# Latent and stick-breaking attention of a four-layer model reordered into one loop of heads, and the layer norms' scale and bias moved from POOL to ACT

## The reference, cut to what matters

```python
# first_block: layer 0 gated delta net + conv FFN, layer 1 short convolution + conv FFN
h = layer_norm(ALPHA * h + mix, ln_mix_g[i], ln_mix_b[i])
h = layer_norm(ALPHA * h + conv_ffn(h, ...), ln_ffn_g[i], ln_ffn_b[i])
# second_block, layer 0: mixer_mla_sb; layer 1: mixer_fox
h = x @ w_in                                   # c_q 256, c_kv 256, k_rope 32, sb_qkv 3*8*64
q  = rms_norm(c_q, q_norm_g) @ w_uq            # 8 heads of 64 + 32 (rope)
kv = rms_norm(c_kv, kv_norm_g) @ w_ukv         # 8 heads of 64 (k) + 64 (v)
o_a = softmax(q k^T * 96**-0.5, block mask) @ v        # latent attention (MLA), 8 heads
# stick-breaking (SB), 8 heads: z = q k^T / 8, past = s < t
log_rem = where(past, log_sigmoid(-z), 0); between = reverse_cumsum(log_rem) - log_rem
o_b = where(past, exp(log_sigmoid(z) + between), 0) @ v
mix = concatenate([o_a, o_b]) @ w_out
x = layer_norm(DEEPNORM_ALPHA * x + mix, ...); x = layer_norm(DEEPNORM_ALPHA * x + swiglu(x), ...)
x = x + sigmoid(x @ ple_w_gate + ple_b_gate) * (p @ ple_w_proj)
```

## Time and profile before

| | |
|---|---|
| median of 3 runs | 1532.27 us (1530.16 to 1534.51) |
| profiled execution, its own time | 1531.54 us |
| its span, first to last instruction | 1529.7 us |
| mean granted TensorE clock | 0.973 of full speed |
| busy: PE, DVE, ACT, POOL | 1428.1, 1062.2, 917.5, 416.3 us |
| attention stage, 777.6 to 910.9 us | 133.3 us |
| one weight unit from issue to landing | 3.7 us (median of 419) |

### The profile page before, as it was taken

The page is one execution under the profiler, slowest core; times in us unless marked ns, Lnnn a source line. Parts: engine busy times, 40 slices in busy tenths (PEclk is TensorE's granted clock), DMA queues, the critical chain, the costliest instruction groups (busy, mean ns, idle before and its releaser), DMA issues.

```text
span 1529.7 us, 30955 instructions
## 1 busy us (share of the span) xinstructions
PE 1428.1 (93%) x11068; PEld 1370.9 (90%) x11068; DVE 1062.2 (69%) x1682; ACT 917.5 (60%) x1535; POOL 416.3 (27%) x427
## 2 busy tenths in 40 slices
PE   6989988999999999999988789999998989999997
PEld 6889978999999999998977669999998968999997
DVE  7776645888748978886487627765567755866557
ACT  5622345555685475557756657556865876655864
POOL 4122000632205306322062004512037020722005
PEclk9989998999999999999999899999999999999999
DMA  5422214455564564555635105655645532555562
GB/s 202 148 73 87 66 52 128 129 176 179 158 203 136 175 196 145 171 180 176 199 120 163 58 14 163 197 178 179 200 144 152 168 108 84 179 178 192 181 191 83
DMA packets 62725, 226.00 MB, mean 148 GB/s; under 512 B 6960, under 2 KB 8240, under 8 KB 62640
## 3 DMA queue, kind: packets, MB, share of 16 engines
q1 hardware_dynamic: 61776, 221.87, 46.9%
q10 hardware_dynamic: 864, 3.01, 0.6%
HBM read 223.80 MB, written 1.05 MB: 147 GB/s over the span
## 4 chain that ended last, share of the span: by engine, by line
PE 61%; DVE 22%; issue 6%; ACT 6%; POOL 3%; DMA 1%; DVEq 1%; SPq 0%; ACTq 0%
PE bank L393 16%; PE bank L394 16%; PE bank L395 16%; DVE w_lo L1536 8%; DVE cv L1894 2%; POOL h L2164 2%; DVE x_lo L1572 1%; ACT w_hi L1034 1%; DVE r L1631 1%; POOL h L2162 1%; ACT unused L1021 1%; DVE tu L1596 1%; DVE tg L1596 1%; DVE r L1576 1%; PE bank L903 1%
## 5 line engine op out<-in xcount | busy, mean ns | idle before, releaser
L393 PE MATMUL bank<-x_hi,w_hi 128*128 128x258 f32 (+5 forms) x2144 | 621.1, 290 | 31.0 <-DVE w_lo L1536 15.7
L395 PE MATMUL bank<-x_hi,w_lo 128*128 128x258 f32 (+5 forms) x2144 | 611.1, 285 | 0.0
L394 PE MATMUL bank<-x_lo,w_hi 128*128 128x258 f32 (+5 forms) x2144 | 611.1, 285 | 0.0
L393 PEld LDWEIGHTS bank<-x_hi,w_hi 128*128 128x128 f32 x2144 | 409.1, 191 | 40.3 <-issue 20.6
L1536 DVE TENSOR_TENSOR w_lo<-raw,w_hi 128x1024 fp32r<-128x1024 f32 x299 | 392.1, 1325 | 49.1 <-ACT w_hi L1034 34.6
L394 PEld LDWEIGHTS bank<-x_lo,w_hi 128*128 128x128 f32 x2144 | 409.8, 191 | 0.5
L395 PEld LDWEIGHTS bank<-x_hi,w_lo 128*128 128x128 f32 x2144 | 409.2, 191 | 0.0
L1034 ACT ACTIVATE w_hi<-raw 128x1024 fp32r<-128x1024 f32 x299 | 313.4, 1053 | 120.0 <-PE bank L395 100.9
L1534 DVE SCALAR_TENSOR_TENSOR w_lo<-raw,negmean,w_hi 128x1024 fp32r<-128x1024 f32 x120 | 155.5, 1299 | 151.8 <-ACT w_hi L1032 150.6
L393 PE MATMUL bank<-a_hi,w_hi 128*128 (+2 forms) x704 | 199.1, 283 | 6.2 <-DVE w_lo L1534 6.1
L395 PE MATMUL bank<-a_hi,w_lo 128*128 (+2 forms) x704 | 198.8, 282 | 0.0
(11 more groups left out here) (410 smaller groups left out, 2169.7 us busy)
## 6 DMA issues: line engine op xcount, KB each, us to landing
raw<-w SPq DMA_DIRECT2D x419, 512.0 KB, 3.7
h<-h SPq DMA_DIRECT2D x2, 544.0 KB, 6.6
out<-h SPq DMA_DIRECT2D x8, 128.0 KB, 1.9
T<-cs ACTq DMA_DIRECT2D x1, 960.0 KB, 5.1
con_b<-cb ACTq DMA_DIRECT2D x1, 712.0 KB, 4.1
smx<-pin ACTq DMA_DIRECT2D x1, 512.0 KB, 5.0
con_g<-ca ACTq DMA_DIRECT2D x1, 421.5 KB, 8.0
prm<-par ACTq DMA_DIRECT2D x1, 202.0 KB, 4.6
```

Source lines behind the costliest of these rows:

```text
L393: pe.matmul(o, wh, xh, start=first, stop=False)
L394: pe.matmul(o, wh, xl, start=False, stop=False)
L395: return pe.matmul(o, wl, xh, start=False, stop=last)
```

## The change

It has two parts.

**The attention stage.** The kv latent comes before the q latent in `m_in` and in the norms, and `m_ukn` before `m_uq` (host-side order of the weights). x3 is written to buffers of its own, `y3_hi` and `y3_lo`; POOL scales its tiles 4 to 7 (`ln_times`) and DVE 0 to 3, in the order `X3_ORDER`. The split of p (`p_hi`, `p_lo`) moves from before the stage to the start of norm 1. The rope of k comes after the low halves, its copy to eight heads goes from DVE to POOL; the latents' deviations, reciprocals and splits move between the q and k units. `m_sbv` is accumulated in `misc[0..1]`, so v is copied from there; `m_ukn` and `m_uq` go into half banks, k is copied by DVE in four operations, q by ACT in four, and q's rope is three DVE operations for four heads (`q_ropes`). The two attentions become one loop: round i has the scores of MLA head i+1, the sums of SB head i+1, z of SB head i+2, the value product of SB head i, the transpose of MLA head i and the value product of MLA head i-1. SB uses `misc[0..1]` and `acc[0..1]`, MLA `misc[2]` (scores), `misc[3]` (transpose) and `acc[2..3]`. The first units of `m_out` are averaged and split within the loop, and `row_stage(4)` takes the tiles in the order `M_ORDER`, in which they are finished. One activation table serves both attentions and is loaded in the q and k units.

**The layer norms.** `keep` on POOL makes only `r * rstd`. Scale and bias are an ACT activation, `gain_and_bias`, at fixed places: two in each of the first four pairs of an up phase, two in each of the first four tiles of the short convolution, one in each gate unit. In `pair` on ACT the row mean moves behind the first tap.

The diff, cut to its core:

```diff
 (PE)
-            first_pair(U["m_sbqk"], SEQ, "x3", list(range(KT)), U["m_sbqk"] - 3)
...
-            panels(U["m_sbqk"] + 2, 6, SEQ)
+            first_pair(U["m_sbqk"], SEQ, "x3", X3_ORDER, U["m_sbqk"] - 3, y3)
+            c_sums(0)
+            panels(U["m_sbqk"] + 2, 2, SEQ, None, y3)
+            c_sums(1)
+            panels(U["m_sbqk"] + 4, 4, SEQ, None, y3)
             mean_of_h(4, SEQ)
+            pe.wait_ge(S("c_std"), 2)
+            tokens(U["m_sbv"], KT, y3_hi, y3_lo, misc)
+            four(U["m_ukn"], c_hi[:, 0:2, :], c_lo[:, 0:2, :], halves_of(misc[2:4]))
...
+            four(U["m_uq"], c_hi[:, 2:4, :], c_lo[:, 2:4, :], halves_of(acc[0:2]))
+            four(U["m_uq"] + 1, c_hi[:, 2:4, :], c_lo[:, 2:4, :], halves_of(acc[2:4]))
+            sb_z(0)
+            pe.wait_ge(S("k_copied"), 1)
+            tokens(U["m_ukv"], 2, c_hi[:, 0:2, :], c_lo[:, 0:2, :], misc[2:4])
+            sb_z(1)
+            sb_sums(0)
+            pe.wait_ge(S("k_rope"), 1)
+            mla_scores(0)
+            for i in range(9):
+                if i + 1 < 8:
+                    mla_scores(i + 1)
+                    sb_sums(i + 1)
+                if i + 2 < 8:
+                    sb_z(i + 2)
+                if i < 8:
+                    sb_times_v(i)
+                    mla_turn(i)
+                if i:
+                    mla_times_v(i - 1)
+            row_stage(4, SEQ, mixed)
 (ACT)
+            def gain_and_bias(n, k, N):
+                scaled_n[0] += 1
+                act.wait_ge(S("ln_h1"), scaled_n[0])
+                A(h[:, k, 0:N], h[:, k, 0:N], ACT.Identity, bias=par_col(f"ln_b{n}", k), scale=par_col(f"ln_g{n}", k)).then_inc(S("ln_h"), 1)
...
                 def pair(u, s, j):
                     act.wait_ge(S("unit_done"), u + 1)
-                    ahead(u, s)
+                    split(u + RING, s + RING)
                     act.wait_ge(S("ffn_tu"), jb + 1)
...
                         A(cv[:, par, 0:M], tu[:, par, 0:M], ACT.Copy, scale=par_col(conv, j * 3)).then_inc(S("ffn_tap0"), 1)
+                        row_mean(u + (RING + 1), s + RING + 1)
                         act.wait_ge(S("ffn_taps"), j + (cbase + 1))
...
                     ahead(u + 1, s + 1)
+                    if isinstance(j, int) and j < KT // 2:
+                        gain_and_bias(2 * ups[0], 2 * j, N)
+                        gain_and_bias(2 * ups[0], 2 * j + 1, N)
...
+            for i in range(9):
+                if i + 1 < 8:
+                    sb_soft(i + 1)
+                if i < 8:
+                    mla_exp(i)
+                    sb_att(i)
+                if 1 <= i < 4:
+                    row_mean(U["m_out"] + i, U["m_out"] + i)
+                    split(U["m_out"] + i, U["m_out"] + i)
+                if i == 4:
+                    row_mean(U["m_out"] + 4, U["m_out"] + 4)
+                if i:
+                    mla_copy(i - 1)
+                if i >= 2 and i % 2 == 0:
+                    sb_high(i // 2 - 1)
+                if i >= 3 and i % 2:
+                    mla_high(i // 2 - 1)
...
                     if i == 0 and m >= 2:
                         y_copy(m - 2)
+                    gain_and_bias(n, m, SEQ)
                     act.wait_ge(S("gate_t"), KT * i + m + 1)
 (DVE)
+            def q_ropes(j):
+                q, t = q_m[:, 4 * j:4 * j + 4, :], q_t[:, 4 * j:4 * j + 4, :]
...
+                dve.wait_ge(S("q_copied"), j + 1)
+                link(V.tensor_tensor(t[rope_rows], q[swap_rows], turn(swap_rows), ALU.mult))
+                link(V.tensor_tensor(q[rope_rows], q[rope_rows], turn(rope_rows), ALU.mult))
+                V.tensor_tensor(q[rope_rows], q[rope_rows], t[rope_rows], ALU.add).then_inc(S("q_rope"), 1)
...
+            q_ropes(0)
+            sb_remains(0)
+            mla_max(0)
+            for i in range(9):
+                if i + 1 < 8:
+                    sb_remains(i + 1)
+                if i < 8:
+                    mla_norm(i)
+                if i == 0:
+                    q_ropes(1)
+                if 1 <= i < 4:
+                    ahead(U["m_ukn"] + i, U["m_ukn"] + i)
+                if i + 1 < 8:
+                    mla_max(i + 1)
+                if i >= 2 and i % 2 == 0:
+                    mixed_low(4 + i // 2 - 1, acc[(i // 2 - 1) % 2])
+                if i >= 3 and i % 2:
+                    mixed_low(i // 2 - 1, acc[2 + (i // 2 - 1) % 2])
 (POOL)
             def keep(n, k, N):
                 G.tensor_tensor(h[:, k, 0:N], r[:, k, 0:N], rstd[:, 0:N], ALU.mult).then_inc(S("ln_h1"), 1)
-                pool.wait_ge(S("ln_h1"), KT * kept[0] + k + 1)
-                G.tensor_scalar(h[:, k, 0:N], h[:, k, 0:N], par_col(f"ln_g{n}", k), par_col(f"ln_b{n}", k), ALU.mult, ALU.add).then_inc(S("ln_h"), 1)
...
+            for k in range(4, KT):
+                G.tensor_tensor(r[:, k, 0:SEQ], r[:, k, 0:SEQ], rstd[:, 0:SEQ], ALU.mult).then_inc(S("ln_times"), 1)
+            for k in range(4, KT):
+                pool.wait_ge(S("ln_times"), k - 3)
+                G.tensor_scalar(h[:, k, 0:SEQ], r[:, k, 0:SEQ], par_col("ln_g3", k), par_col("ln_b3", k), ALU.mult, ALU.add).then_inc(S("ln_h"), 1)
...
+            G.tensor_copy(k_m[64:96, :, :], rope_t[64:96, 0, :].unsqueeze(1).to_broadcast([32, 8, SEQ])).then_inc(S("k_rope"), 1)
```

More of the change, by code:

```diff
@@ L300, in v_banks, with halves_of @@
             return [acc[first % RING], acc[(first + 1) % RING]]
+        def halves_of(pair):
+            return [pair[m // 2][:, (m % 2) * SEQ:(m % 2) * SEQ + SEQ] for m in range(4)]
         def blocks(t, lv, side):
@@ L1259, in up_phase @@
                 act.preload_act_table_set("silu_and_others")
-                with act.Fori(0, 6) as i:
+                for j in range(KT // 2):
+                    pair(u0 + 2 * j, u0 + 2 * j, j)
+                with act.Fori(0, 4) as i:
                     for b in range(2):
-                        pair(i * RING + (u0 + 2 * b), u0 + 2 * b, i * 2 + b)
+                        pair(i * RING + (u0 + 8 + 2 * b), u0 + 8 + 2 * b, i * 2 + (4 + b))
                 mean_read(2 * ups[0] + 1, N)
@@ L1350, in _ @@
                 ahead(u, u)
-            A(v_s[:, 0, :], acc[0][:, :], ACT.Copy).then_inc(S("acc_used"), 2)
-            A(v_s[:, 1, :], acc[1][:, :], ACT.Copy).then_inc(S("acc_used"), 2)
+            act.wait_ge(S("acc_used"), U["m_sbv"])
+            A(v_s[:, 0, :], misc[0][:, :], ACT.Copy).then_inc(S("acc_used"), 2)
+            A(v_s[:, 1, :], misc[1][:, :], ACT.Copy).then_inc(S("acc_used"), 2)
+            act.wait_ge(S("unit_done"), U["m_ukn"] + 1)
+            split(U["m_out"], U["m_out"])
             for j in range(2):
@@ L1998, in _, with x3_scaled @@
-            for k in range(KT):
+                times_rstd(smx[:, j, :], u, u, SEQ).then_inc(S("acc_used"), 1)
+            def x3_scaled(k):
+                V.scalar_tensor_tensor(out=r[:, k, 0:SEQ], in0=r[:, k, 0:SEQ], scalar=par_col("ln_g3", k), in1=rstd[:, 0:SEQ], op0=ALU.mult, op1=ALU.mult).then_inc(S("ln_scaled"), 1)
+            c_raw(0)
+            c_raw(1)
+            x3_scaled(0)
+            x3_scaled(1)
+            ahead(U["m_in"] + 1, U["m_in"] + 1)
+            x3_scaled(2)
+            x3_scaled(3)
@@ L2022, in _ @@
                 ahead(u, u)
[L2023 to L2039 removed]
+                if j in (2, 5):
+                    c_over(j // 3)
@@ L2040, in _ @@
+            dve.wait_ge(S("unit_done"), U["m_ukn"] + 1)
+            for i in range(2):
+                for odd in range(2):
+                    v = V.tensor_copy(k_m[0:64, 4 * i + odd:4 * i + odd + 3:2, :], misc[2 + i][64 * odd:64 * odd + 64, :].rearrange("p (a n) -> p a n", a=2))
+            v.then_inc(S("k_copied"), 1)
             ahead(U["m_ukn"], U["m_ukn"])
-            ahead(U["m_ukv"], U["m_ukv"])
-            dve.wait_ge(S("k_rope"), 1)
-            dve.sem_inc(S("m_ready"), 1)
+            q_ropes(0)
```

345 lines of the change are left out of this document (199 added, 146 removed).

## The result

The changed kernel takes 1505.01 us (median of 4 runs, 1503.77 to 1506.98) against 1531.22 (1529.97 to 1534.51): 26.2 us less, ratio 0.9826, 95% interval 0.981 to 0.9842. The profiled execution has a span of 1502.0 us against 1529.7, 27.7 less, and a mean granted clock of 0.979 against 0.973. Forecast were 40 us less, 1492, in a range of 1481 to 1508.

What follows compares the result with a forecast made beforehand. PE, busy 93%, was taken to bound the kernel, so only its waits and slow clock could shrink. Savings of 29.5 + 3 + 4.5 + 3 = 40 us gave 1492 us, range 1481 to 1508.

Steps and rivals of the forecast that it cites:

- the attention stage: From the preceding norm to the first row of m_out: earlier x3, latent projections and one loop of heads save 29.5 us.
- rival D: In x3, POOL's multiplications are held longer beside DVE and pace it; low halves come 3 us later: 1495; chance 0.08.
- The 2 us we put in for overlooked waits: Attention stage: deducted from the 31.5 us saving for waits that following the engines' queues overlooks, leaving 29.5.
- the 40.3 us: Attention stage: waits and slow clock within its 133.3 us, beside 93 of work; the most the rework can give there.
- A: Loop of heads: rounds go by latency, 6.3 us a head instead of 5.2, and the clock falls to 0.84: 1507; chance 0.15.
- E: Loop of heads: a head's pass is fully serial, so the kernel gets slower, 1536; chance 0.03.
- B: PE paces everything with waits almost nil: 9 us less than forecast, 1483; chance 0.13.
- 3 for the up-phase starts and short convolution: Scale and bias on ACT stretch DVE less: 1 us each at two up-phase starts and the short convolution, bounds 0 to 6.6.
- 4.5 for the last pairs' row means: Ends of two convolving up phases: row mean behind the first tap removes PE's weight waits, 4.5 us, bounds 1 and 6.1.
- `p_hi`: nothing, or 1 if not: Second down phase: the split of p (0.95 us) runs three units ahead of PE and costs nothing, or 1 us if not.
- Gates: net 3 in the first, 0 in the last: Gate phases: earlier low parts gain 3 us, a later first sigmoid costs 1.7, less DVE stretch returns 1; bounds 0 to 5.
- Rival C: No side gains: last-pair waits stay with another cause and the gate's table load is paid in full: 1503; chance 0.10.

Runs made afterwards that it cites:

- experiments 6 and 7: Changed kernel with DVE's second q rope moved to round 1: 1501.97 us; changed kernel with row means and splits spread over rounds 1 to 6: 1504.27 us.
- Experiment 3: Changed kernel with the matmuls for the mean of h four units later and ACT's read one tile later: 1502.54 us, ratio 0.9803.
- experiment 8: Changed kernel with ACT's row mean put back ahead of the first tap: 1510.34 us, ratio 0.9876.
- experiment 5: Changed kernel with p_hi moved to the short convolution's fifth tile and p_lo to the start of norm 3: 1505.36 us, ratio 0.983.
- Experiment 2: Changed kernel with the row stage's tile order set to 4, 0, 5, 1, 2, 3, 6, 7: 1502.75 us, ratio 0.9802.
- Experiments 4 and 10: Changed kernel with the sigmoid table loaded ahead of the first scale and bias: 1502.18 us; changed kernel plus six edits, POOL's gate-norm products paced: 1490.56 us.

## Why the prediction came out as it did

The time fell inside the range, 13 us above the forecast. The large term was right, the small ones together were not: 10.5 us forecast, and about 4 lost instead. The range held because the attention stage, three quarters of the sum, came out.

**The attention stage: right.** 29.5 forecast, 30.2 measured. Of its steps, less the 1.3 us by which the stage began ahead: pair done 7.2 sooner (forecast 8.6), value units 11.9 (14), first scores 22.3 (25.1), the loop 39.9 us long (41.4), round 0 6.2 with the stall, rounds 1 to 3 6.0, 4.9 and 5.7 (forecast 6.0 each), the stall behind the second rope 2.53 (2.3), no wait at the row stage. The first three fell short by 1.4, 2.1 and 2.8. The 1.4 can be read on DVE: its scalings of two tiles each take 1.36 and 1.35 and the weight split between them 1.75 while POOL multiplies beside it, where DVE's low halves of the same size take 0.48 each and a split 1.2. That is rival D's mechanism, seen from DVE; no run takes it apart. The 2 us put in for overlooked waits, and a loop 1.5 shorter than forecast, covered it, so that the sum agrees within 0.7 is partly luck. The prediction gives the stage a clock of 0.91 to 0.94; the earlier trace rows has 0.84 in the latent heads and 1.00 in the stick-breaking heads as well, which changes no term, since the 40.3 us were taken as waits and slow clock together. A and E are out: the loop's clock was 0.91 in its first half and 1.00 in its second, and no round was longer than 6.2. B is out: PE alone would have needed 36.2, and experiments 6 and 7 show that 2.1 and 1.9 us of the 3.7 above it hang on DVE's and ACT's places in the loop, not on their work, which is unchanged there.

**"3 for the up-phase starts and short convolution": failed, and it is the largest part of the difference, 5 of 13.** The starts gave +0.8 and +1.1. The short convolution lost 4.0. The bounds were 0 and 6.6, as if this edit could only win. The missed wait: POOL's seven additions for the mean of h start when the last two tiles have their scale and bias, which now happens in ACT's fourth tile, at 504.6; PE's mean stood where it did before, and PE waited 3.35 us and ran at 0.68 of its clock behind it. I had asked who waits for the split behind the new wait on ACT, and not who waits for `ln_h`. Experiment 3 moves those matmuls and ACT's read of them and has 4.0 us back. Norm 1 starts worse as well: eight products of POOL without a pause (476.93) stand beside DVE, two of whose operations take 1.73 us instead of 1.03, and PE waits 2.70 at 483.01 and runs at 0.58 of its clock for 4.0 us. 0.8 of that lies in the stretch to 486, and by 512 the lead is back. This is read from the traces; no run tests it.

**"4.5 for the last pairs' row means": the number was nearly right,** 3.7 in the two phases by experiment 8, **the mechanism only in part.** The prediction took 4.5 of the 6.1 us for which PE waits, and said that no wait over 1 us would be left. Of the waits only 2.0 us went (0.74 and 1.29, then 0.79 and 1.28, are left). Of the other 1.7 some 1.4 came from the clock, which fell to half behind the first phase's waits before and no longer does; the prediction had no such term, so that part was luck. In the second phase, where the clock was 1.00 before too, the same edit gave 1.3. **"`p_hi`: nothing, or 1 if not": it was the second,** 1.4 by experiment 5. The three units between it and PE were no cover, because ACT makes mean and split without a pause there.

**Overlooked: the order of norm 4, 2.5.** The prediction followed `M_ORDER` into the row stage and stopped there. The norm behind it overwrites the tiles in `LAST_ORDER`, and ACT waits until the last unit has read tile 3. Experiment 2.

**"Gates: net 3 in the first, 0 in the last": -1.2 and -0.1.** POOL's low parts do end closer behind DVE's last tile (1.8 us instead of 4.3 from the end of DVE's sum to theirs). But DVE's last tile came 1.8 later, for two reasons: the first sigmoid 1.9 later (table load behind the first scale, forecast 1.7), and DVE's product and sum stretched to 0.95 and 0.84 by eight products of POOL in a row, where the prediction credited 1 for less stretching; the later rounds, 2.63 us for 2.70, give some of it back. Up to the last wait for low parts the phase had still won 0.8. Behind it PE took the next unit at 0.55 of its clock and lost 2.0 against the kernel before, which had met its low parts one by one and had its own half clock earlier, at 1161 to 1168. Experiments 4 and 10 take the first two apart: the first can be mended and gives 1.6 in the two phases, the second only moves.

Rival C named the outcome best, "no side gains", 1503: but not its reasons. The last-pair waits did shrink; the side gains were there, 5.6 us (0.8 and 1.1 at the starts, 3.7 by the row means), and some 9 us of losses stood beside them (4.0, 2.5, 1.4 and 1.3).

What stays open: why the clock takes 1.2 us in one execution and 2.4 in another behind the same wait of the first gate phase, and where the scatter of the first stretch comes from.

## What to carry to other kernels

When work moves from a free engine into fixed places of a full queue, list every consumer of what it makes, not only what stands behind it in the queue: each consumer's old place was chosen for the old producer. When an order of tiles is changed, follow it through the stage behind, which reads or overwrites the same tiles in an order of its own. And lay two traces on each other by the same-numbered instruction: it tells gains and losses of 1 us apart that a median of several runs cannot, as long as no fall of the clock, which scatters by as much, lies between the two instructions.
